# Strassen's method for three slabs of an input projection, in a decoder step on one Trainium2 core

## What is computed

```python
EVEN_IN = 3 * CONV_CH + 2 * SGU_CH        # 5 x 512
def even_mixer(x, conv_prev, w_in, conv_w, sgu_g, sgu_bn, sgu_w, sgu_b, w_out):
    h = x @ w_in                                            # 1024 -> 2560
    gate_b, gate_c, h_in, u, v = jnp.split(h, EVEN_SPLITS, axis=-1)
    conv_out, conv_state = short_conv(gate_c * h_in, conv_prev, conv_w)   # 3 taps over tokens
    y_a = gate_b * conv_out
    v_n = layer_norm(v, sgu_g, sgu_bn)
    s = chunk_mix(v_n, sgu_w, sgu_b)      # per 128 channels: causal 128x128 mix of tokens
    y_b = u * s
    return jnp.concatenate([y_a, y_b], axis=-1) @ w_out, conv_state, v_n
```

## Time and profile before

| | before |
|---|---|
| median of 3 runs | 806.77 us |
| profiled execution, its own time | 809.63 us |
| span of the profile | 807.7 us |
| TensorE matmul busy | 757.3 us (94%) |
| TensorE weight load busy | 526.6 us (65%) |
| VectorE busy | 342.9 us (42%) |
| ScalarE busy | 126.4 us (16%) |
| GpSimd busy | 167.7 us (21%) |
| mean granted TensorE clock | 0.983 |
| HBM traffic | 281 GB/s over the span |

### The profile page before, as it was taken

One profiled execution on the slowest core, in us unless ns is written; L12 is line 12 of the kernel. 1 busy time (PEld: TensorE's weight loads), 2 busy tenths in 40 slices (PEclk: granted clock), 3 DMA queues, 4 the chain that ended last, 5 costly groups with the idle time before them and its releaser, 6 DMA issues.

```text
span 807.7 us, 14630 instructions
## 1 busy us (share of the span) xinstructions
PE 757.3 (94%) x6239; PEld 526.6 (65%) x6239; DVE 342.9 (42%) x826; ACT 126.4 (16%) x333; POOL 167.7 (21%) x265
## 2 busy tenths in 40 slices
PE   6999999999999999999998689999999999979865
PEld 4888878999999999867675347743443344433321
DVE  0164336866777654162597831365023010120107
ACT  0020023111100001131212452151010010000011
POOL 3400377252400000022123631023101101110120
PEclk9999999999999999999998799999999999999998
DMA  8899897999944245999424928949999999999991
GB/s 256 292 355 351 276 290 206 307 297 346 323 144 143 73 144 168 295 292 248 145 105 143 329 80 337 408 173 319 394 410 409 396 395 363 394 395 410 397 398 63
DMA packets 112659, 227.55 MB, mean 282 GB/s; under 512 B 25090, under 2 KB 64330, under 8 KB 109396
## 3 DMA queue, kind: packets, MB, share of 16 engines
q1 hardware_dynamic: 96580, 177.13, 62.1%
q0 software_dynamic: 12080, 42.48, 16.2%
q10 hardware_dynamic: 3936, 7.01, 2.7%
HBM read 203.04 MB, written 23.57 MB: 281 GB/s over the span
## 4 chain that ended last, share of the span: by engine, by line
PE 78%; SPq 7%; DVE 6%; DMA 5%; ACT 2%; issue 1%; POOL 1%; ACTq 0%; DVEq 0%
PE ps L913 24%; PE ps L767 21%; PE ps L1299 13%; SPq L409 6%; PE ps L1327 6%; DMA slot<-moe_w 2%; PE ps L818 2%; DMA slot<-w_in_even 1%; DMA scr<-r_rows,rowk 1%; PE ps L1237 1%; PE ps L994 1%; PE ps L1169 1%; PE ps L1146 1%; PE ps L1117 1%; PE ps L1131 1%
## 5 line engine op out<-in xcount | busy, mean ns | idle before, releaser
L767 PE MATMUL ps<-xw,slot 128*128 128x264 f32 x512 | 125.7, 402 | 6.6 <-DMA slot<-w_in_even 6.6
L1299 PE MATMUL ps<-slot,hT 128*32 128x512 f32 x1056 | 116.4, 593 | 8.3 <-DMA slot<-moe_w 6.8
L767 PEld LDWEIGHTS ps<-xw,slot 128*128 128x128 f32 x512 | 99.0, 196 | 28.0 <-DMA slot<-w_in_even 9.3
L1299 PEld LDWEIGHTS ps<-slot,hT 128*32 128x32 f32 x1056 | 33.8, 110 | 85.8 <-issue 71.5
L913 PE MATMUL ps<-sqT,slot 128*128 128x132 f32 x640 | 78.3, 276 | 0.0
L913 PEld LDWEIGHTS ps<-sqT,slot 128*128 128x128 f32 x640 | 75.0, 190 | 0.0
L1327 PE MATMUL ps<-slot,hT 128*32 128x256 f32 x1216 | 68.3, 380 | 0.9 <-DMA slot<-moe_w 0.9
L913 PE MATMUL ps<-rw,slot 128*128 128x132 f32 x480 | 60.7, 275 | 0.0
L767 PE MATMUL ps<-yT,slot 128*128 128x264 f32 x256 | 59.5, 388 | 0.0
L913 PEld LDWEIGHTS ps<-rw,slot 128*128 128x128 f32 x480 | 57.1, 189 | 0.3 <-ACT rw L1466 0.2
L2332 DVE TENSOR_TENSOR yT<-silu,ps 128x256 f32<-128x256 f32 x19 | 8.0, 422 | 113.7 <-ACT silu L1663 113.7
(11 more groups left out here) (473 smaller groups left out, 957.7 us busy)
## 6 DMA issues: line engine op xcount, KB each, us to landing
slot<-moe_w SPq DMA_DIRECT2D x50, 1024.0 KB, 15.8
slot<-moe_w SPq DMA_DIRECT2D x16, 2048.0 KB, 14.4
slot<-ffn_w SPq DMA_DIRECT2D x22, 1024.0 KB, 13.5
scr<-moe_w SPq DMA_DIRECT2D x14, 1024.0 KB, 17.7
slot<-ffn_w SPq DMA_DIRECT2D x8, 1408.0 KB, 6.2
slot<-w_in_even SPq DMA_DIRECT2D x4, 2048.0 KB, 17.9
r_rows<-silu ACTq DMA_DIRECT2D x1, 6528.0 KB, 33.4
slot<-k_pages SPq DMA_DIRECT2D x6, 1024.0 KB, 6.2
```

Source lines behind the costliest of these rows:

```text
L767: mm = pe.matmul(out, lhs(k), rhs(k), start=(k == 0), stop=(k == n - 1))
L1299: mm = pe.matmul(ps[t][32 * j:32 * j + 32, :].rearrange("p (w n) -> p w n", w=2), xgT[:, cap * k + 32 * t:cap * k + 32 * t + 32], moe_slab ...
```

## The change

Three of the five slabs (`gate_c`, `u`, `gate_b`) are computed in pairs of output tiles by Strassen's method in the form that the feed-forward uses; `v` and `h_in` stay plain. A pair is tiles j and j+2 of a slab (j = 0, 1), so there are six pairs, p = 0 to 5. VectorE makes four sums of the token halves once (`token_sums`, into `tsum`) and four of the weight blocks for each pair (`in_weights`, into `rw` for even pairs and `cache` for odd ones, one of them in place in the slab). TensorE makes the seven products in `in_pair`, the first three into one bank, the rest into a second bank and `ps[6]` or `ps[7]`. ScalarE copies the first product (`copy_in_p`), and VectorE assembles the two tiles in `in_first` and `in_second`. The last four mixings come in twos behind the pairs of `gate_b`, the copy of the transposed `v` goes to ScalarE, the output projection takes `yT` in another order and waits for its rows by a counter `y_ready`.

```diff
+        MIXED = (0, 2, 4, 5, 1, 3, 6, 7)
+        E_PAIRS = ((1, 0), (1, 1), (3, 0), (3, 1), (4, 0), (4, 1))
@@ TensorE
+            def in_pair(p, mid=None):
+                (a11, a12, s3, a22), (s1, s2, s4) = in_quarters(p), in_sums(p)
+                xlo, xhi = xT[:, :, 0:HT], xT[:, :, HT:T]
+                b = bank()
+                part_product(b[:, 0:HT], a11, xlo[:, 0:4])
+                part_product(b[:, HT:2 * HT], a12, xlo[:, 4:8])
+                pe.wait_ge(wsum_done, p + 1)
+                pe.wait_ge(tsum_done, 4)
+                done.inc(part_product(b[:, 2 * HT:3 * HT], s2, tsum[:, 1]))
+                if mid:
+                    mid()
+                b = bank()
+                part_product(ps[6 + p % 2][:, 0:HT], s4, xhi[:, 4:8])
+                part_product(b[:, HT:2 * HT], s1, tsum[:, 0])
+                part_product(b[:, 2 * HT:3 * HT], s3, tsum[:, 2])
+                done.inc(part_product(b[:, 0:HT], a22, tsum[:, 3]))
...
+                if n in (1, 3):
+                    arrived(s)
+                    for j in range(2):
+                        in_pair(n - 1 + j)
...
+            arrived(S_EIN[4])
+            in_pair(4, mid=turn_v)
+            mix(0)
+            mix(1)
+            in_pair(5)
+            mix(2)
+            mix(3)
...
-                    ready = (lambda k: (group_free, G_MIX + k + 1)) if c == 0 else None
+                    ready = (lambda k: (y_ready, k + 1)) if c == 0 else None
@@ ScalarE
+            def copy_in_p(p):
+                act.wait_ge(group_done, in_group(p) + 1)
+                act.copy(in_p[:, p % 2], ps[in_group(p) % NB][:, 0:HT]).then_inc(p1_copied, 1)
+
+            copy_in_p(0)
+            copy_in_p(1)
             act.wait_ge(even_in, 16 * 7)
             act.wait_ge(pool_consts, 5)
             norm(4, vT, vT, V_SG, V_SB)
...
+            copy_in_p(2)
+            copy_in_p(3)
+            copy_in_p(4)
+            act.wait_ge(vt_done, 1)
+            for t in range(2):
+                act.copy(vtok[:, t, :], ps[4 + t][:, :]).then_inc(vt_copied, 1)
+            copy_in_p(5)
@@ VectorE
+            def in_weights(p):
+                dve.wait_ge(slab_in[S_EIN[E_PAIRS[p][0]]], 16)
+                (a11, a12, a21, a22), (s1, s2, s4) = in_quarters(p), in_sums(p)
+                link(V.tensor_tensor(s1, a21, a22, ALU.add))
+                mark(V.tensor_tensor(a21, a11, a21, ALU.subtract))
+                link(V.tensor_tensor(s2, s1, a11, ALU.subtract))
+                V.tensor_tensor(s4, a12, s2, ALU.subtract).then_inc(wsum_done, 1)
+
+            def in_first(p):
+                b, z = filled(), hT[:, in_tiles(p), :]
+                dve.wait_ge(p1_copied, p + 1)
+                free.inc(V.tensor_tensor(z[:, :, 0:HT], twice(in_p[:, p % 2]), blocks(b, 1), ALU.add))
+
+            def in_second(p):
+                b, z = filled(), hT[:, in_tiles(p), :]
+                dve.wait_ge(group_free, free.k)
+                link(V.tensor_tensor(z[:, :, HT:T], twice(z[:, 1, 0:HT]), blocks(b, 1), ALU.add))
+                mark(V.tensor_tensor(halves(z[:, 1, :]), twice(z[:, 1, HT:T]), blocks(b, 0), ALU.add))
+                free.inc(V.tensor_tensor(z[:, 0, HT:T], z[:, 0, HT:T], ps[6 + p % 2][:, 0:HT], ALU.add))
+
+            token_sums(xT[:, :, 0:HT], xT[:, :, HT:T], tsum_done)
             for c in range(4):
                 free.inc(V.tensor_copy(hT[:, 16 + c, :], filled()[:, 0:T]))
-            for c in range(4):
-                free.inc(V.tensor_copy(hT[:, 4 + c, :], filled()[:, 0:T]))
-            dve.wait_ge(even_in, 16 * 7)
-            norm(4, hT[:, 16:20, :])
+            in_weights(0)
+            in_first(0)
+            in_weights(1)
+            in_second(0)
+            in_first(1)
             dve.wait_ge(idx_in, 16 * 16)
...
+            in_second(1)
...
+            in_weights(2)
...
             V.tensor_copy(zlast[:, :, 0:2], zext[:, :, 256:258]).then_inc(z_done, 1)
-            for c in range(4):
-                free.inc(V.tensor_copy(hT[:, 12 + c, :], filled()[:, 0:T]))
...
+            norm(4, hT[:, 16:20, :])
+            in_first(2)
+            in_weights(3)
+            in_second(2)
+            in_first(3)
+            in_weights(4)
+            in_second(3)
...
+            in_first(4)
+            in_weights(5)
+            in_second(4)
+            dve.wait_ge(x_ready, 4)
+            gated_rows(0)
+            mixed_row(0)
+            mixed_row(1)
+            in_first(5)
+            in_second(5)
+            gated_rows(1)
+            mixed_row(2)
+            mixed_row(3)
```

More of the change, by code:

```diff
@@ L357, in moe_slab, with in_quarters, in_sums, in_group @@
             return where.rearrange("p (k n) -> p k n", k=4)
+        P1_DOWN = len(E_PAIRS) + KF - 2 * PLAIN
+        def in_quarters(p):
+            n, j = E_PAIRS[p]
+            v = slab(S_EIN[n], KD, 512)
+            return [v[:, k:k + 4, c + P * j:c + P * j + P] for c, k in ((0, 0), (0, 4), (256, 0), (256, 4))]
+        def in_sums(p):
+            v = (flat(rw), cache)[p % 2][:, 0:1536].rearrange("p (q k n) -> p q k n", q=3, k=4)
+            return [v[:, q] for q in range(3)]
+        def in_group(p):
+            n, j = E_PAIRS[p]
+            return G_EIN + 16 + 4 * j if n == 4 else G_EIN + 4 * n + 2 * j
+        def in_tiles(p):
+            n, j = E_PAIRS[p]
+            return {1: slice(4 + j, 7 + j, 2), 3: slice(12 + j, 15 + j, 2), 4: slice(2, 4)}[n]
         def up_views(s):
@@ L839, in _, with part_product @@
             y = lambda k: yT[:, k, :]
-            for n, s in enumerate(S_EIN[0:4]):
-                for j in range(4):
+            def part_product(out, lhs, rhs):
+                for k in range(4):
+                    mm = pe.matmul(out, lhs[:, k], rhs[:, k, :], start=(k == 0), stop=(k == 3))
+                return mm
+            def in_pair(p, mid=None):
[14 more added lines that the diff above has]
+                done.inc(part_product(b[:, 0:HT], a22, tsum[:, 3]))
+            for n, s in enumerate(S_EIN[0:4]):
+                if n in (1, 3):
+                    arrived(s)
+                    for j in range(2):
+                        in_pair(n - 1 + j)
+                for j in range(4 if n in (0, 2) else 0):
                     if n == 0 and j == 1:
@@ L854, in _, with turn_v, mix @@
                     for c in range(4):
[L855 to L858, removed]
-                        for c in range(4):
[L860 to L875, removed]
+                        stats(c, 4, hT[:, 16:20, :], yT, (group_free, G_EIN + c + 1))
+            def turn_v():
+                pe.wait_ge(x_ready, 4)
+                for t in range(2):
+                    for c in range(4):
+                        mm = pe.transpose(ps[4 + t][:, P * c:P * c + P], hT[:, 16 + c, P * t:P * t + P], ident)
+                mm.then_inc(vt_done, 1)
+            def mix(j):
+                pe.wait_ge(vt_copied, 2)
+                pe.wait_ge(causal_w, 1)
+                b = bank()
+                for t in range(2):
+                    mm = pe.matmul(b[:, P * t:P * t + P], vtok[:, t, P * j:P * j + P], wsT[:, j, :],
+                                   start=True, stop=True)
+                done.inc(mm)
+            arrived(S_EIN[4])
[5 more added lines that the diff above has]
+            mix(3)
             def tails():
@@ L885, in tails @@
                 mm.then_inc(z_t, 1)
-            mixed = [4 * mix + j for mix, j in MIX_ORDER]
             for n, sl in enumerate(S_EOUT):
@@ new lines, in in_second @@
+            def in_second(p):
[4 more added lines that the diff above has]
+                free.inc(V.tensor_tensor(z[:, 0, HT:T], z[:, 0, HT:T], ps[6 + p % 2][:, 0:HT], ALU.add))
+            for i in range(4):
+                dve.wait_ge(x_in[i], 32)
@@ new lines, in _, with gated_rows, mixed_row @@
+            in_first(2)
[4 more added lines that the diff above has]
+            in_second(3)
+            def gated_rows(j):
+                dve.wait_ge(group_free, free.k)
+                for a in range(2):
+                    V.tensor_tensor(yT[:, j + 2 * a, :], hT[:, 2 + a, :], hT[:, 8 + j + 2 * a, :],
+                                    ALU.mult).then_inc(y_ready, 1)
+            def mixed_row(g):
+                b = filled()
+                mark(V.tensor_scalar(css, hT[:, 16 + g, TP:T], w00[:, 0, g:g + 1], w00[:, 1, g:g + 1],
+                                     ALU.mult, ALU.add))
+                free.inc(V.tensor_tensor(cst.rearrange("p (t i) -> p t i", t=2),
```

66 lines of the change are left out of this document (32 added, 34 removed).

## The result

The changed kernel takes 814.41 us (median of 4 runs, 814.34 to 814.69), the kernel before 806.01 (4 runs: the three behind the 806.77 of above and one of 805.26). The ratio is 1.0095, 95% interval 1.0068 to 1.0122: slower by about 1%. Measured once more beside the other experiments it took 813.44 us (6 runs, 811.57 to 815.07) against 806.81 (17 runs), ratio 1.0085, interval 1.0069 to 1.0100. The span of its profile is 812.5 us against 807.7.

What follows compares the result with a forecast made beforehand. TensorE was taken to bound the kernel: -4.5 (pairs) + 1.3 + 6.5 + 0.3 (waits) = +3.6, plus 1.7 for the clock = +5.3 us. Forecast median 812.1 us, range 809.2 to 815.8.

Steps and rivals of the forecast that it cites:

- What bounds: TensorE without a break from 14.87 us through the feed-forward; shifts at its first out-projection group reach the end one to one.
- the stages behind 100 us give the shift back: Sign of being wrong: stages after the first out-projection group, expected shifted and alike, would return the loss; no size given.
- rival (c): Attention's low-clock stretches fall otherwise, each 3.4 us less giving back 1.7: not slower; chance 0.12.
- The gain of the pairs: Six pairs in three slabs, 28 matmuls of 0.2275 us each: 6.37 instead of 7.12 us, saving 4.5 us.
- The holes: TensorE waits 1.3 us at pair 0, 6.5 at pair 3, 0.3 for the output projection's last y row.
- The clock: Behind pair 3's hole, one 3.4 us stretch at 1.2 GHz: +1.7 us, bounds 0 and 3.4.
- rival (b): Clock falls twice: pair 0's 1.3 us wait costs a stretch, or pair 3's stretch doubles; 813.8, both 815.5; chance 0.13.
- Rival (a): Clock holds through pair 3's hole, as at 724.44: +3.6 us, 810.4 us; chance 0.18.
- The total: Whole kernel: +5.3 us, so 814.9 us for the profiled execution and a median of 812.1 us.

Runs made afterwards that it cites:

- the filled version: Changed kernel, with TensorE repeating pair 3's first product seven times (28 matmuls) while it waits for pair 3's sums; 809.26 us, ratio 1.0011 to 1.0058.

## Why the prediction was right, point by point

**What bounds.** Right. The stage is TensorE's, and its shift arrives: behind it the long feed-forward chain starts at 147.17 instead of 140.92, 6.25 us later, which is 6.95 less 0.7 by which this execution had begun pair 0 earlier. The feed-forward passes it on whole: from the end of the stage to the end of the feed-forward are 243.0 us in all ten profiles. The span is only 4.8 us longer, though, so a sign that I had named for being wrong, that the stages behind 100 us give the shift back, is there in part. From the end of the feed-forward to the first matmul of the experts the profile of before has 202.4 us and that of the change 200.4, at a mean clock of 0.94 and 0.96. That looks like rival (c), but it was an accident of the one profile of before: the kernel before with the late normalisation, whose stage is the same, has 200.5 there, and the second profile of the change 200.4. So no run shows that the change gives anything back. The spans of these last two profiles differ by 4.9 us and their stages by 5.9; the medians of the later runs, 813.44 against 806.81, differ by 6.6.

The kernel before, attention and routing, busy time by stretch:

```profile
345.00:529.00 184.00, 167.68 (x999) 115.98 (x998) 98.92 (x287) 56.14 (x165) 48.69 (x62) 0.94 0.71 236
```

The changed kernel, nearly the same work:

```profile
351.00:533.50 182.50, 165.87 (x1000) 115.34 (x999) 99.18 (x287) 56.42 (x166) 48.61 (x62) 0.96 0.73 239
```

**The gain of the pairs.** A little too small: 4.5 forecast, 4.9 measured. The step that was off is the 0.2275 us a matmul, taken from 17.52 us for 77; that interval holds a start behind other matmuls and the tail of its last record. The 55 matmuls in its middle, 312.23 to 324.61, take 0.225 each. Uninterrupted, pair 2 took 6.29 us, 0.2246 each, against 0.445 / 2 = 0.2225.

**The holes.** Forecast 1.3, 6.5 and 0.3; the brackets show 1.38, 6.76 and 0.39. What they cost is somewhat more, 1.64, 6.93 (with another 0.1 that is counted with the clock) and 0.66. The bracket begins where the last record ends, 0.16 us behind the pace of the work, and the first matmuls behind a wait take 0.11 longer (1.01 us instead of 0.90 for the four at 30.67). I had not counted that: 0.27 us a hole. Pairs 1, 2, 4 and 5 had no hole, as said. The sums of 512 columns took 0.68 to 0.69 (estimate 0.685).

**The clock.** The mechanism was right, the size was not. I took one stretch of 3.4 us at 1.2 GHz, all of it behind the hole, 1.7 lost. The stretch was 6.7 us long in both profiles of the change. That is the second branch of rival (b), a stretch twice as long, to which I gave 0.13 together with the first. It did not cost the 3.4 us of that rival either, 2.65 in the one execution and 1.57 in the other, because it began inside the hole, some 5 us behind its start in the first profile and some 3 in the second. What costs is half of that part of it in which TensorE has work. Rival (a), the clock holds, did not happen: the granted clock fell in every profile with this hole. The other branch of rival (b), pair 0's 1.4 us hole brings a fall too, did not happen in these profiles.

**The total.** Forecast 812.1 in 809.2 to 815.8; measured 814.41 and 813.44, nearer to rival (b)'s 813.8. The account at the out-projection was +5.3 against +6.95: 0.95 more by the clock, 0.4 by the long hole, 0.3 and 0.4 by the other two, less 0.4 by the pairs. The profiled execution took 814.44, where 814.9 was forecast; that is luck, since its stage was 1.65 us longer than forecast and the profile of before had an attention 2 us longer than its like. Against the first medians the change costs 8.4 us and not 5.3; the stage explains 6.95 of them in one profile and 5.87 in the other, and for the rest no run gives a cause.

**What I did not see:** that the loss is a matter of order and can be won back. The prediction counted the columns of VectorE's queue one behind the other and never asked whether the sums of pair 3 could stand elsewhere. Their inputs (the slab, and `cache`) were there long before: the version with early sums began them at 49.55 without a wait for either, 22 us before the 71.61 of the change.

## What to carry to other kernels

Fewer multiplications on the bounding engine make new inputs that another engine must deliver in time. Count for each of them when it is wanted, when its own inputs are there, and what stands ahead of it in the producer's queue; a job with no one waiting (here a normalisation) does no harm until something urgent is put behind it. A hole of several microseconds in TensorE's stream is priced with the clock: half of the time that TensorE works at the lower level comes on top of the hole, if the clock falls.

## What the runs showed of the hardware that was not expected

- The clock fell in holes of 3.74 and 6.76 us, but in the same place not behind two of 1.06 and 2.06; in the kernel before it stayed at 1.00 behind one of 3.08. Under the same hole of 6.76 us the loss was 1.57, 2.65 and (behind 6.75) 3.02 us in three profiles. One cannot forecast it to better than about a microsecond from the rows. The Trainium skill (TensorE: Matmul & The Clock Gate, Part 1: The HAM clock gate) has the fall after idleness; these runs agree with it for 6.76 us of idleness, and the filled version shows it as a cause.
- A start behind a wait costs TensorE some 0.27 us beyond the idle time that the bracket shows (1.38 in the bracket of pair 0 and 1.64 in its length; 0.39 and 0.66 at the output projection).
- One kernel's executions differ by over 3 us (the changed kernel's ten by 3.5). Over the ten profiles of all these kernels the time from the end of the stage to the end of the feed-forward is the same within 0.02 us, while attention with routing takes 198.7 to 202.4 us and the experts 267.2 to 269.4, though their work is the same in all of them. The granted clock suggests that its falls there are the reason, which no run shows. The two profiles alone put this change at +4.8 us, the first medians at +8.4, the later ones at +6.6.
